# The down projections of two feed-forward blocks and of the last MLP in blocks of 1024 inner by seven half-size products

## The chip, the cores and the metric

The kernel runs on one core of one Trainium2 chip. The metric is the device time of one execution in microseconds (us); the median of three runs is given. A profile of one execution comes with it. The engines are PE (matrix products), DVE (vector), ACT (activation), POOL (GpSimd) and SP, which only issues loads.

## The reference

The reference takes 512 tokens of width 1024 through a state-space mixer, a feed-forward block (FFN), a sparse attention, a second FFN, a hybrid attention, a cross attention and a last MLP. What the change touches is the second matrix product of each of the three feed-forward parts, in float32:

```
gate, up = split(h @ w_gate_up); x = x + (silu(gate) * up) @ w_down     inner width 2816, twice
x = x + relu(h @ w_up)**2 @ w_down_2                                    inner width 4096, once
```

The output width of all three is 1024, so the down weights have 22, 22 and 32 tiles of 128 inner rows.

## The kernel before

**Numbers.** PE takes float32 in a rounded form. Every operand is split in two parts: hi is the value rounded, lo is the rest. `three` (L2180 to L2185) makes one tile of a product by three matmuls: hi by hi, lo of the weights by hi, hi by lo of the activations. All of them run on line L2183.

**Slots.** Weights pass in slots of 128 x 2048 through a pair of buffers: SP loads a slot into `raw` (L456 to L461, two DMAs of 512 KB), ACT rounds it into `w_hi` (L942), POOL subtracts and writes `w_lo` (L682), PE uses it. ACT's rounding of slot g waits for `w_used`, PE's end with slot g - 2; SP's load of slot g waits for the split of slot g - 2. At each of four places where POOL is busy with a norm, DVE splits the slot instead (L1650). Slots are counted in one row through the whole program, 145 of them.

**Up projections.** `t_slot` (L2207) makes 2 output tiles of 128 x 512 (transposed: inner by tokens) with 48 matmuls of 512 columns. In an FFN, one slot gives gate and up of one inner tile: ACT takes silu (L1089), DVE multiplies (L1705), rounds into `hT_hi` (L1707) and subtracts into `hT_lo` (L1709). In the MLP a slot gives two inner tiles: ACT takes relu twice (L1402, L1404), DVE squares 128 x 1024 (L1997), rounds (L1999) and subtracts (L2001). The MLP does 16 inner tiles up, then all 16 down, and this twice (parts); an FFN does 22 up, then 22 down. These loops are hardware loops of two slots (`Fori`).

**Down projections.** `n_slot` (L2187) takes a slot of 3 or 4 inner tiles by 512 output columns; for each of 4 blocks of 128 tokens it makes 3 matmuls per inner tile into one PSUM bank (4 to 7). First all slots of output columns 0 to 511 (a panel), then those of 512 to 1023: 12 slots in an FFN (`FFN_DOWN`), 8 in each part of the MLP. After a panel DVE adds the four banks to the residual `x_res` (L1688).

**The end of an FFN.** The last slot (`n_slot_halves`, L2260) is woven with the next norm. `norm_halves` on DVE (L1645) first splits the next stage's first slot (L1650), then adds token block 0, and so on; ACT squares each block (L986), POOL makes the reciprocal root (L694, L695), DVE and ACT scale the two halves of the block (L1626, L1002), and PE turns it (`half_turn`, L2256) behind blocks 2 and 3 of the last slot. ACT and DVE then copy the turned block into `xT_hi` (L1017) and `xT_lo` (L1641), on which the next stage's first matmuls wait.

**Order.** Each engine works through its own list in order; the order is written out by hand and kept by semaphores.

Of the kernel before, what the change touches and what calls it, by code (L numbers as in the profile page):

```python
# [17 lines left out]
F32R = mybir.dt.float32r  # L18
# [5 lines left out]
P = 128  # L24
# [43 lines left out]
def shape_constants():  # L68
# [61 lines left out]
def program(nc, w, out):  # L130

    with ExitStack() as ctx:
# [44 lines left out]
        sink_e = fixed("sink_e", [P, 8])  # L177
        PS = ctx.enter_context(nc.psum_tensor("PS", [P, 8, 512], F32))
# [2539 lines left out]
```

## Time and profile before

| | |
|---|---|
| median of 3 runs | 1944.69 us (1942.04, 1944.69, 1945.69) |
| the profiled execution: span from the first to the last instruction | 1941.7 us |
| PE busy | 1906.7 us, 98% of the span |
| DVE, ACT, POOL busy | 749.7, 738.5, 811.6 us |
| mean granted TensorE clock | 0.993 |

The profiled execution has no device time of its own on record; its span lies 0.3 us below the fastest and 4.0 us below the slowest of the three runs, and 3.0 us below their median. The profile gives each instruction's start and duration. A matmul's record is longer than its turn: consecutive matmuls overlap, so their pace is read from the distance of their starts, not from the mean duration. Some matmul records can be missing.

### The profile page before, as it was taken

Reading aid. Unit: us, or ns where it says so; the run is one execution under the profiler, and the core shown is the slowest. Engines: PE = TensorE matmul, PEld = TensorE weight load, DVE = VectorE, ACT = ScalarE, POOL = GpSimd, SP = SyncE. Lnnn points to the kernel's source line nnn. Section 1 sums busy time; section 2 is a strip of 40 time slices with the busy share of each in tenths; the row PEclk is TensorE's granted clock in tenths of the full one; section 3 lists DMA queues with packets and bytes.
Section 4 is the critical chain, followed back from the end, with each engine's and each line's share of the span. In section 5 each row is a group of like instructions: output and inputs, shape, how many; then the busy total and the mean of one; then the engine's idle time right before and its main releaser. Section 6 shows DMA issues by size and latency. Waiting matters only on the chain.

```text
span 1941.7 us, 24992 instructions
## 1 busy us (share of the span) xinstructions
PE 1906.7 (98%) x9667; PEld 1541.1 (79%) x9667; DVE 749.7 (39%) x1286; ACT 738.5 (38%) x1141; POOL 811.6 (42%) x411
## 2 busy tenths in 40 slices
PE   7999999999999999999999999999999999999998
PEld 5778888888888878768888888888776778888887
DVE  8973321111003377982211110021636556403721
ACT  6624343222123244683432221243457462212221
POOL 1004344444443458553343434433345444443433
PEclk9999999999999899999999999999999999999999
DMA  6423323332332222103333333335120223323231
GB/s 161 95 51 133 109 77 97 91 103 76 102 103 73 87 65 87 66 2 87 88 86 108 87 95 99 114 86 157 55 66 23 79 64 90 105 88 107 86 108 65
DMA packets 210205, 170.84 MB, mean 88 GB/s; under 512 B 19658, under 2 KB 174746, under 8 KB 210058
## 3 DMA queue, kind: packets, MB, share of 16 engines
q1 hardware_dynamic: 207954, 166.19, 29.2%
q10 hardware_dynamic: 2168, 3.52, 0.5%
q8 instruction: 55, 0.90, 0.2%
q14 instruction: 28, 0.23, 0.0%
HBM read 162.58 MB, written 2.65 MB: 85 GB/s over the span
## 4 chain that ended last, share of the span: by engine, by line
PE 90%; DVE 4%; ACT 4%; issue 1%; DMA 1%; POOL 1%; SPq 0%; POOLq 0%; DVEq 0%; ACTq 0%
PE PS L2183 77%; PE PS L2473 2%; PE PS L2464 2%; PE PS L2483 2%; DMA xp<-in_x 1%; PE PS L2079 1%; PE PS L2100 1%; PE PS L2080 1%; PE PS L2112 1%; DVE taken L1935 1%; PE PS L2426 0%; PE PS L2121 0%; PE PS L2256 0%; ACT probs_t L1232 0%; PE PS L2129 0%
## 5 line engine op out<-in xcount | busy, mean ns | idle before, releaser
L682 POOL TENSOR_TENSOR w_lo<-raw,w_hi 128x2048 fp32r<-128x2048 f32 x141 | 652.0, 4624 | 832.1 <-ACT w_hi L942 830.6
L942 ACT ACTIVATE w_hi<-raw 128x2048 fp32r<-128x2048 f32 x145 | 277.9, 1917 | 630.1 <-PE PS L2183 630.1
L2183 PE MATMUL PS<-xT_hi,w_hi 128*128 128x512 f32 (+1 forms) x1152 | 441.1, 383 | 2.4 <-DVE xT_lo L1641 1.3
L2183 PE MATMUL PS<-xT_lo,w_hi 128*128 128x512 f32 (+1 forms) x1152 | 438.2, 380 | 0.0
L2183 PE MATMUL PS<-xT_hi,w_lo 128*128 128x512 f32 (+1 forms) x1152 | 438.1, 380 | 0.0
L2183 PEld LDWEIGHTS PS<-xT_hi,w_hi 128*128 128x128 f32 x1152 | 216.6, 188 | 49.0 <-issue 7.9
L2183 PEld LDWEIGHTS PS<-xT_lo,w_hi 128*128 128x128 f32 x1152 | 216.6, 188 | 41.5
L2183 PEld LDWEIGHTS PS<-xT_hi,w_lo 128*128 128x128 f32 x1152 | 216.7, 188 | 40.1
L2183 PE MATMUL PS<-w_hi,hT_hi 128*128 128x512 f32 x608 | 236.9, 390 | 0.0
L2183 PE MATMUL PS<-w_hi,hT_lo 128*128 128x512 f32 x608 | 236.6, 389 | 0.0
L2183 PE MATMUL PS<-w_lo,hT_hi 128*128 128x512 f32 x608 | 236.5, 389 | 0.0
L2183 PE MATMUL PS<-w_hi,xT_hi 128*128 128x512 f32 (+2 forms) x592 | 232.0, 392 | 0.9 <-ACT ki_raw L1146 0.7
L2183 PE MATMUL PS<-w_hi,xT_lo 128*128 128x512 f32 (+2 forms) x592 | 228.6, 386 | 0.0
L2183 PE MATMUL PS<-w_lo,xT_hi 128*128 128x512 f32 (+2 forms) x592 | 228.4, 386 | 0.0
L1705 DVE TENSOR_TENSOR gbuf<-gbuf,PS 128x512 f32<-128x512 f32 x44 | 30.3, 689 | 378.8 <-PE PS L2183 378.8
L2183 PEld LDWEIGHTS PS<-w_hi,xT_hi 128*128 128x128 f32 x592 | 114.4, 193 | 29.2 <-issue 8.9
L1688 DVE TENSOR_TENSOR x_res<-x_res,PS 128x512 f32<-128x512 f32 x40 | 27.4, 686 | 279.8 <-PE PS L2183 279.8
L2183 PEld LDWEIGHTS PS<-w_hi,hT_lo 128*128 128x128 f32 x608 | 114.1, 188 | 23.8
L2183 PEld LDWEIGHTS PS<-w_lo,hT_hi 128*128 128x128 f32 x608 | 114.2, 188 | 23.6
L2183 PEld LDWEIGHTS PS<-w_hi,hT_hi 128*128 128x128 f32 x608 | 114.1, 188 | 23.4
L2183 PEld LDWEIGHTS PS<-w_hi,xT_lo 128*128 128x128 f32 x592 | 114.4, 193 | 21.1
L2183 PEld LDWEIGHTS PS<-w_lo,xT_hi 128*128 128x128 f32 x592 | 114.6, 194 | 19.9
(338 smaller groups left out, 2026.2 us busy)
## 6 DMA issues: line engine op xcount, KB each, us to landing
raw<-in_ffn_w_gate_up SPq DMA_DIRECT2D x88, 512.0 KB, 4.6
raw<-in_ffn_w_down SPq DMA_DIRECT2D x40, 512.0 KB, 4.4
raw<-in_w_up SPq DMA_DIRECT2D x32, 512.0 KB, 5.0
raw<-in_w_down SPq DMA_DIRECT2D x32, 512.0 KB, 4.3
raw<-in_dsa_w_in SPq DMA_DIRECT2D x28, 512.0 KB, 4.5
raw<-in_w_in SPq DMA_DIRECT2D x21, 512.0 KB, 4.3
raw<-in_s_w_glu SPq DMA_DIRECT2D x16, 512.0 KB, 4.5
raw<-in_dsa_w_o SPq DMA_DIRECT2D x8, 512.0 KB, 4.6
```

Source lines behind the costliest of these rows:

```text
L682: pool.tensor_tensor(w_lo[:, par, :], raw[:, par, :], f32(w_hi[:, par, :]), ALU.subtract).then_inc(w_split, 1)
L942: act.activation(w_hi[:, par, :], raw[:, par, :], ACT.Copy).then_inc(w_rounded, 1)
L1688: tt(x_res[:, tb, cols], x_res[:, tb, cols], PS[:, 4 + tb, :], ALU.add).then_inc(n_free, 1)
L1705: tt(gbuf[:, pair, 1, :], gbuf[:, pair, 0, :], PS[:, 2 * pair + 1, :], ALU.mult).then_inc(t_free, 1)
L1935: tt(lg[:, :, 0:cols - 1], lg[:, :, 0:cols - 1], rest[:, :, 1:cols], ALU.mult).then_inc(st_prob, 1)
L2079: mm(o, uT[:, GB * b + g, :], tp[:, g, :, :].rearrange("p t h -> p (t h)"), start=True, stop=False)
L2080: ins = mm(o, states[:, g, :], out_a[b % 3][:, g, 1:CH + 1, :].rearrange("p t h -> p (t h)"), start=False, stop=True)
L2100: mm(o, b_n[:, GB * b + g, :], out_a[b % 3][:, g, 0:CH, :].rearrange("p t h -> p (t h)"), start=g % 4 == 0, stop=False)
L2183: ins = mm(o, a if weights_stay else c, c if weights_stay else a, start=first and n == 0, stop=last and n == 2)
L2464: mm(PS[:, dot_bank(u0, t), 0:k.shape[1]], q[half:half + HD], k[half:half + HD], start=True, stop=True).then_inc(col_dot, 1)
L2473: ins = tr(PS[:, 4 + e % 2, P * j:P * j + P], probs[:, e % ring, P * j:P * j + P], ident[:, :])
L2483: ins = mm(PS[HD * i:HD * i + HD, 6 + (p // 4) % 2, at:at + P], units[2 * p + i][3][j], probs_t[:, 2 * (p % 2) + i, P * j:P * j + P], star ...
```

## The change

The inner width is taken in blocks of 8 tiles (1024): two blocks in each FFN (6 tiles are left), three in the MLP (8 tiles are left), seven in all. For a block, tokens (512) are halved, inner (1024) is halved and output columns (1024) are halved. The plain way takes 8 products of 256 tokens x 512 inner x 512 columns; here 7 are taken of sums of the quarters (the scheme of Strassen in the form with 4 sums on each side). A product is 24 matmuls of 128 x 128 by 512 columns (2 token blocks x 4 inner tiles x 3). The tiles that are left over go the old way, in 4 slots per FFN (3 tiles each) and 4 in the MLP (4 tiles each).

- **Where.** A block's 7 products stand between two up slots: the block's last up slot, then one more up slot, then products 0 to 6, then the next up slot. In an FFN a block spans 8 up slots, in the MLP 4. The MLP is no longer in two parts.
- **Loads.** The raw down weights of a block (4 DMAs of 1 MB, `dn_load`) go to a buffer of their own. The first of them waits, from the second block on, until the block before has been split.
- **Weights.** Products 0, 3 and 5 take a raw quarter: ACT rounds it in two halves of 128 x 1024, POOL splits it in two halves. Products 1, 2, 4 and 6 take a sum of quarters: DVE makes the sum (128 x 2048) and splits it, ACT rounds it. The up slot after product 6 is split by DVE (`first_split`), not POOL.
- **Activations.** For each pair of inner tiles DVE makes four sums of 128 x 256 (`pair_sums`), ACT rounds seven pieces of 128 x 256 (`pair_round`: 512, 256 and 1024 wide), DVE subtracts them (`pair_rest`, the same widths).
- **Results.** After each product DVE adds its two banks to `x_res` (`dn_add`, 14 a block). Products 2, 4, 5 and 6 accumulate on a bank that holds an earlier product, so they wait until that one has been added.
- **Loops.** The hardware loops of the three parts are written out. `g_last` has a place of its own; slot numbers shift; `raw` is counted without the products.

The core of the diff (12 columns of indentation are left out):

```diff
-FFN_SLOT = [8, 61]
-FFN_DOWN = [3, 3, 4, 4, 4, 4]
+FFN_RUN, FFN_DN = 8, 2
+FFN_LAST = [3, 3]
+DSA_SLOT = 48
+def up_slot(g0, j, run, dns):
+    return g0 + j + DN * sum(j > run * (c + 1) for c in range(dns))
+def raw_of(g):
+    return g - DN * sum(g > first for first in DN_FIRST)
+DN_PRODUCTS = ("raw", "sum", "sum", "raw", "sum", "raw", "sum")
+DN_QUARTER = {0: (0, 0), 3: (1, 0), 5: (1, 1)}
+DN_SUM = {1: 0, 2: 1, 4: 2, 6: 3}
+DN_ROWS = (0, 3, 4, 1, 5, 6, 2)
+DN_BANK = (4, 6, 4, 0, 4, 6, 4)
+DN_FRESH = (True, True, False, True, False, False, False)
+DN_INTO = ((0, 0), (1, 1), (0, 1), (0, 0), (1, 1), (0, 1), (1, 0))
+DN_BEHIND = (None, None, 0, None, 2, None, 4)
...
-hT_hi = place("hT_hi", "arena", 0, [P, FT, S], F32R)
-hT_lo = place("hT_lo", "arena", FT * S * 4, [P, FT, S], F32R)
-gbuf = place("gbuf", "spare", 0, [P, 2, 2, 512])
+hs_hi = place("hs_hi", "arena", 0, [P, 4, DN, 256], F32R)
+hs_lo = place("hs_lo", "arena", 28 * KB, [P, 4, DN, 256], F32R)
+hT_hi = place("hT_hi", "arena", 16 * KB, [P, 8, S], F32R)
+hT_lo = place("hT_lo", "arena", 32 * KB, [P, 8, S], F32R)
+dn_raw = place("dn_raw", "arena", 56 * KB, [P, 4, 2, 2, 512])
+hid = place("hid", "spare", 0, [P, 2, 512])
+silu = place("silu", "spare", 4 * KB, [P, 2, 512])
+mlp_hid = [hid, silu]
+h_sum = place("h_sum", "spare", 8 * KB, [P, 4, 256])
+sum_b = place("sum_b", "spare", 4 * KB, [P, 4, 512])
...
+def dn_load(cc, src, m):
+    if m == 0 and cc:
+        sp.wait_ge(dn_lo_pool, 6 * cc)
+        sp.wait_ge(dn_sum, 4 * cc)
+    sp.dma_start(dn_raw[:, m, :, :, :].rearrange("p j l n -> p j (l n)"), src).then_inc(dn_ld, 16)
...
+def dn_split(cc, i):
+    g, (j, l) = DN_FIRST[cc] + i, DN_QUARTER[i]
+    for half in range(DN_HALF):
+        ms = slice(2 * half, 2 * half + 2)
+        hi, lo = (t[:, g % 2, 1024 * half:1024 * half + 1024].rearrange("p (m n) -> p m n", n=512) for t in (w_hi, w_lo))
+        pool.wait_ge(dn_hi, 14 * cc + 2 * i + half + 1)
+        pool.tensor_tensor(lo, dn_raw[:, ms, j, l, :], f32(hi), ALU.subtract).then_inc(dn_lo_pool, 1)
...
+def up_splits(g0, run, dns, ups, chunk):
+    for j in range(2, ups):
+        c, at = divmod(j, run)
+        if at == 1 and 1 <= c <= dns:
+            for i in (0, 3, 5):
+                dn_split(chunk + c - 1, i)
+        else:
+            split_run(up_slot(g0, j, run, dns), 1)
...
+def dn_round(cc, i):
+    g = DN_FIRST[cc] + i
+    act.wait_ge(w_used, g - 1)
+    if DN_PRODUCTS[i] == "raw":
+        act.wait_ge(dn_ld, 64 * (cc + 1))
+    else:
+        act.wait_ge(dn_sum, 4 * cc + DN_SUM[i] + 1)
+    for half in range(DN_HALF):
+        ms = slice(2 * half, 2 * half + 2)
+        if DN_PRODUCTS[i] == "raw":
+            src = dn_raw[:, ms, DN_QUARTER[i][0], DN_QUARTER[i][1], :]
+        else:
+            src = (sum_b if DN_SUM[i] % 2 else sum_a)[:, ms, :]
+        act.activation(w_hi[:, g % 2, 1024 * half:1024 * half + 1024].rearrange("p (m n) -> p m n", n=512), src,
+                       ACT.Copy).then_inc(dn_hi, 1)
...
+def pair_round(kk, h):
+    m = kk % 4
+    act.activation(hs_hi[:, m, 0:2, :], h[:, :, 0:256], ACT.Copy)
+    act.activation(hs_hi[:, m, 2, :], h[:, 1, 256:512], ACT.Copy).then_inc(hs_rounded, 1)
+    act.wait_ge(hs_sum, kk + 1)
+    act.activation(hs_hi[:, m, 3:DN, :], h_sum[:, :, :], ACT.Copy).then_inc(hs_rounded, 1)
...
+        next_round(g + 2)
+        if c < FFN_DN and j % 2:
+            act.wait_ge(t_free, t0 + j + 3)
+            pair_round(4 * (c0 + c) + at // 2, hid)
+        if at == 0 and 1 <= c <= FFN_DN:
+            dn_rounds(g0, FFN_RUN, j)
+    g0 += FT + DN * FFN_DN
+    m = len(FFN_LAST)
+    round_run(g0 + 2, m)
     norm_early(1 + 2 * layer, n_free, TB * (FFN_PANEL[layer] + 2))
...
+def pair_sums(kk, h):
+    if kk:
+        dve.wait_ge(hs_rounded, 2 * kk)
+    tt(h_sum[:, 0, :], h[:, 0, 256:512], h[:, 1, 256:512], ALU.add).then_inc(v_step, 1)
+    steps[0] += 1
+    tt(h_sum[:, 2, :], h[:, 0, 0:256], h[:, 0, 256:512], ALU.subtract)
+    dve.wait_ge(v_step, steps[0])
+    link(tt(h_sum[:, 1, :], h_sum[:, 0, :], h[:, 0, 0:256], ALU.subtract))
+    tt(h_sum[:, 3, :], h[:, 1, 0:256], h_sum[:, 1, :], ALU.subtract).then_inc(hs_sum, 1)
+def pair_rest(kk, h):
+    m = kk % 4
+    dve.wait_ge(hs_rounded, 2 * kk + 1)
+    tt(hs_lo[:, m, 0:2, :], h[:, :, 0:256], f32(hs_hi[:, m, 0:2, :]), ALU.subtract)
+    tt(hs_lo[:, m, 2, :], h[:, 1, 256:512], f32(hs_hi[:, m, 2, :]), ALU.subtract)
+    dve.wait_ge(hs_rounded, 2 * kk + 2)
+    dve.wait_ge(hs_sum, kk + 1)
...
+def dn_first_sum(cc):
+        dve.wait_ge(dn_lo_dve, 8 * cc)
...
+def dn_rest(cc, i):
+    g, src = DN_FIRST[cc] + i, sum_b if DN_SUM[i] % 2 else sum_a
+    dve.wait_ge(dn_sum, 4 * cc + DN_SUM[i] + 1)
+    for half in range(DN_HALF):
+        ms = slice(2 * half, 2 * half + 2)
+        hi, lo = (t[:, g % 2, 1024 * half:1024 * half + 1024].rearrange("p (m n) -> p m n", n=512) for t in (w_hi, w_lo))
+        dve.wait_ge(dn_hi, 14 * cc + 2 * i + half + 1)
+        tt(lo, src[:, ms, :], f32(hi), ALU.subtract).then_inc(dn_lo_dve, 1)
...
+def dn_add(cc, i):
+    rows, col = DN_INTO[i]
+    for t in range(2):
+        if t == 0:
+            dve.wait_ge(dn_first, DN * cc + i + 1)
+        else:
+            dve.wait_ge(w_used, DN_FIRST[cc] + i + 1)
+        xs = x_res[:, 2 * rows + t, 512 * col:512 * col + 512]
+        tt(xs, xs, PS[:, DN_BANK[i] + t, :], ALU.add).then_inc(dn_added, 1)
...
+def dn_dve(cc):
+    dve.wait_ge(dn_sum, 4 * cc + 1)
+    dve.wait_ge(hs_done, 4 * cc + 4)
+    tt(sum_b[:, :, :], dn_raw[:, :, 1, 1, :], sum_a[:, :, :], ALU.subtract).then_inc(dn_sum, 1)
+    dn_rest(cc, 1)
+    dn_add(cc, 0)
+    dn_rest(cc, 2)
+    dve.wait_ge(dn_lo_dve, 8 * cc + 2)
+    tt(sum_a[:, :, :], dn_raw[:, :, 1, 1, :], dn_raw[:, :, 0, 1, :], ALU.subtract).then_inc(dn_sum, 1)
+    dn_add(cc, 1)
+    dve.wait_ge(dn_lo_dve, 8 * cc + 4)
+    tt(sum_b[:, :, :], dn_raw[:, :, 1, 0, :], sum_b[:, :, :], ALU.subtract).then_inc(dn_sum, 1)
+    dn_add(cc, 2)
+    dn_rest(cc, 4)
+    dn_add(cc, 3)
+    dn_add(cc, 4)
+    dn_rest(cc, 6)
+    dn_add(cc, 5)
+    first_split(DN_FIRST[cc] + DN)
+    dn_add(cc, 6)
...
-                  norm=6 if part and i else None)
+for j in range(MLP_UP):
+    h = mlp_hid[j % 2]
+    c, at = divmod(j, MLP_RUN)
+    dve.wait_ge(t_free, MLP_TILE + j + 3)
+    tt(h[:, :, :], h[:, :, :], h[:, :, :], ALU.mult).then_inc(hid_made, 1)
+    if at == 0 and 1 <= c <= MLP_DN:
+        dn_dve(MLP_CHUNK + c - 1)
+    dve.wait_ge(hid_made, j + 1)
+    if c < MLP_DN:
+        pair_sums(4 * (MLP_CHUNK + c) + at, h)
+        pair_rest(4 * (MLP_CHUNK + c) + at, h)
+        if at == MLP_RUN - 1:
+            dn_first_sum(MLP_CHUNK + c)
...
+def dn_pe(cc, pair):
+    for i in range(DN):
+        g, c = DN_FIRST[cc] + i, DN_ROWS[i]
+        par = g % 2
+        if i == 0:
+            pe.wait_ge(hs_done, 4 * cc + 4)
+            if cc:
+                pe.wait_ge(dn_added, 14 * cc)
+            pe.wait_ge(n_free, pair[1])
+        if DN_BEHIND[i] is not None:
+            pe.wait_ge(dn_added, 14 * cc + 2 * DN_BEHIND[i] + 2)
+        if i == 3:
+            pe.wait_ge(t_free, pair[0])
+        for half in range(DN_HALF):
+            if DN_PRODUCTS[i] == "raw":
+                pe.wait_ge(dn_lo_pool, 6 * cc + 2 * (0, 3, 5).index(i) + half + 1)
+            else:
+                pe.wait_ge(dn_lo_dve, 8 * cc + 2 * DN_SUM[i] + half + 1)
+            for t in range(2):
+                for m in (2 * half, 2 * half + 1):
+                    cols, rows = slice(512 * m, 512 * m + 512), slice(P * t, P * t + P)
+                    ins = three(PS[:, DN_BANK[i] + t, :], w_hi[:, par, cols], w_lo[:, par, cols],
+                                hs_hi[:, m, c, rows], hs_lo[:, m, c, rows], False,
+                                DN_FRESH[i] and m == 0, DN_FRESH[i] and m == 3, not DN_FRESH[i])
+                if half:
+                    ins.then_inc(w_used if t else dn_first, 1)
...
```

## Rows read from the trace of the kernel before

**Rows 1.** Page, parts 1 and 2: busy time; busy tenths and granted clock in 40 slices

```profile
PE 1906.7 (98%) x9667; PEld 1541.1 (79%) x9667; DVE 749.7 (39%) x1286; ACT 738.5 (38%) x1141; POOL 811.6 (42%) x411
PEclk9999999999999899999999999999999999999999
```

**Rows 2.** Chain of waits in order of time: start, us, what

```profile
251.63 353.38 PE PS L2183 x1590
...
1586.26 348.44 PE PS L2183 x1536
```

**Rows 3.** Groups by form, PE: shapes, count, busy us, mean ns, idle before

```profile
L2183 PE MATMUL PS<-w_hi,hT_hi 128*128 128x512 f32 x608 | 236.9, 390 | 0.0
```

**Rows 4.** Timeline, POOL, the MLP's first slots: start, duration, line, operation

```profile
1599.92 4.69 POOL L682 TENSOR_TENSOR w_lo<-raw,w_hi 128x2048 fp32r<-128x2048 f32 x1 [4.06 <-ACT w_hi L942]
1610.80 4.68 POOL L682 TENSOR_TENSOR w_lo<-raw,w_hi 128x2048 fp32r<-128x2048 f32 x1 [6.19 <-ACT w_hi L942]
```

**Rows 5.** Timeline, DVE, the same stretch

```profile
1598.07 1.22 DVE L1997 TENSOR_TENSOR gbuf<-gbuf 128x1024 f32<-128x1024 f32 x1 [7.35 <-ACT gbuf L1404]
...
1600.27 5.42 DVE L2001 TENSOR_TENSOR hT_lo<-gbuf,hT_hi 128x1024 f32 x1
```

**Rows 6.** Groups by form, DVE: count, busy us, mean ns

```profile
L1709 DVE TENSOR_TENSOR hT_lo<-gbuf,hT_hi 128x512 f32 x44 | 30.5, 693 | 5.4
L1650 DVE TENSOR_TENSOR w_lo<-raw,w_hi 128x2048 fp32r<-128x2048 f32 x4 | 9.2, 2292 | 124.4 <-ACT w_hi L942 124.4
```

**Rows 7.** One line's instructions: duration ns min/median/max (L1676, L942, L682)

```profile
L1676 DVE TENSOR_TENSOR x_res<-x_res,glu_v x16: 424/426/3625, 171.5 to 246.3; 128x256 f32<-128x256 f32 x16
L942 ACT ACTIVATE w_hi<-raw x145: 1894/1916/2003, 148.1 to 1913.0; 128x2048 fp32r<-128x2048 f32 x145
L682 POOL TENSOR_TENSOR w_lo<-raw,w_hi x141: 4517/4623/4940, 150.1 to 1915.0; 128x2048 fp32r<-128x2048 f32 x141
```

**Rows 8.** Timeline, ACT: relu of one tile, turned tiles (six of 128x256)

```profile
1597.44 0.60 ACT L1404 ACTIVATE gbuf<-PS 128x512 f32<-128x512 f32 x1
608.14 2.28 ACT L1017 ACTIVATE xT_hi<-PS,gains 128x256 fp32r<-128x256 f32 x6
```

**Rows 9.** Timeline, PE and DVE, end of a token block in the first FFN

```profile
602.12 0.39 PE L2183 MATMUL PS<-w_hi,hT_hi 128*128 128x512 f32 x1
602.33 0.69 DVE L1688 TENSOR_TENSOR x_res<-x_res,PS 128x512 f32<-128x512 f32 x1 [0.54 <-PE PS L2183]
```

**Rows 10.** Timeline, POOL and DVE, 614 to 620 us

```profile
614.86 4.61 POOL L682 TENSOR_TENSOR w_lo<-raw,w_hi 128x2048 fp32r<-128x2048 f32 x1 [2.64 <-ACT w_hi L942]
616.33 3.23 DVE L1641 SCALAR_TENSOR_TENSOR xT_lo<-PS,gains,xT_hi 128x256 fp32r<-128x256 f32 x8 [3.08 <-ACT xT_hi L1017]
```

**Rows 11.** Timeline, ACT and DVE, the last slot of the first FFN

```profile
596.94 1.92 ACT L942 ACTIVATE w_hi<-raw 128x2048 fp32r<-128x2048 f32 x1 [8.96 <-PE PS L2183]
598.89 2.29 DVE L1650 TENSOR_TENSOR w_lo<-raw,w_hi 128x2048 fp32r<-128x2048 f32 x1 [50.28 <-ACT w_hi L942]
601.10 0.68 DVE L1688 TENSOR_TENSOR x_res<-x_res,PS 128x512 f32<-128x512 f32 x1
603.68 0.71 ACT L1002 ACTIVATE x_n<-x_res,rstd 128x512 f32<-128x512 f32 x1
607.52 0.72 ACT L1002 ACTIVATE x_n<-x_res,rstd 128x512 f32<-128x512 f32 x1 [0.41 <-POOL rstd L695]
```

**Rows 12.** Chain of waits around the same slot's end

```profile
605.01 0.87 PE PS L2256 x8
...
608.32 1.40 PE PS L2183 x6
...
609.98 2.97 PE PS L2183 x12
```

**Rows 13.** DMA issues by line: count, KB each, median us to landing

```profile
raw<-in_w_up SPq DMA_DIRECT2D x32, 512.0 KB, 5.0
w_kv<-in_w_xkv SPq DMA_DIRECT2D x2, 1024.0 KB, 7.6
```

More of the change, by code:

```diff
@@ new lines, in _ @@
+            for j in range(MLP_UP):
+                g = up_slot(MLP_SLOT, j, MLP_RUN, MLP_DN)
+                slot_free(g)
+                load_pair(raw_of(g) % 2, up[:, :, 2 * P * j:2 * P * j + P], up[:, :, 2 * P * j + P:2 * P * j + 2 * P], P)
+                c, m = divmod(j - 1, MLP_RUN)
+                if 0 <= c < MLP_DN:
+                    dn_load(MLP_CHUNK + c, down[:, 8 * c + 2 * m:8 * c + 2 * m + 2, :], m)
+            g = MLP_SLOT + MLP_UP + DN * MLP_DN
+            for i in range(2):
+                k = 8 * MLP_DN
+                for m in MLP_LAST:
+                    slot_free(g)
+                    load_rows(raw_of(g) % 2, down[:, k:k + m, 512 * i:512 * i + 512], 512)
+                    k += m
+                    g += 1
@@ L799, in _ @@
             split_run(XO_SLOT + 2, 1)
[L800 to L805 removed]
+            up_splits(MLP_SLOT, MLP_RUN, MLP_DN, MLP_UP, MLP_CHUNK)
+            split_run(MLP_SLOT + MLP_UP + DN * MLP_DN, 2 * len(MLP_LAST))
             norm_rstd(6)
@@ new lines, in dn_rounds @@
+            def dn_rounds(g0, run, j):
+                c = j // run - 1
+                for i in range(DN):
+                    next_round(dn_slot(g0, c, i, run) + 2)
+            def ffn_act(layer):
+                g0, t0, c0 = FFN_SLOT[layer], FFN_TILE[layer], FFN_CHUNK[layer]
+                for j in range(FT):
+                    n, g = FT * layer + j, up_slot(g0, j, FFN_RUN, FFN_DN)
+                    c, at = divmod(j, FFN_RUN)
+                    act.wait_ge(t_first, t0 + j + 1)
+                    if j >= 2:
+                        act.wait_ge(t_free, t0 + j + 1)
+                    if at == 1 and 1 <= c <= FFN_DN:
+                        act.wait_ge(dn_lo_dve, 8 * (c0 + c))
+                    act.activation(silu[:, j % 2, :], PS[:, 2 * ((t0 + j) % 2), :], ACT.Silu).then_inc(hid_act, 1)
+                    next_round(g + 2)
[4 more added lines that the diff above has]
+                        dn_rounds(g0, FFN_RUN, j)
+                g0 += FT + DN * FFN_DN
+                m = len(FFN_LAST)
+                round_run(g0 + 2, m)
@@ L2365, in ffn_pe @@
             def ffn_pe(layer, n, j0, freed):
-                g0, t0, h0 = FFN_SLOT[layer], FFN_TILE[layer], FFN_HID[layer]
+                g0, t0 = FFN_SLOT[layer], FFN_TILE[layer]
                 t_slot_halves(g0, g0 % 2, t0, n, j0, freed)
-                t_slot(g0 + 1, (g0 + 1) % 2, t0 + 1, 1, xT_hi, xT_lo)
-                with pe.Fori(0, FT // 2 - 1) as i:
-                    for j in range(2):
-                        t_slot(i * 2 + (g0 + j + 2), (g0 + j) % 2, i * 2 + (t0 + j + 2), (t0 + j) % 2, xT_hi, xT_lo)
@@ L2372, in ffn_pe @@
-                g0 += FT
-                m = len(FFN_DOWN)
+                for j in range(1, FT):
+                    c, at = divmod(j, FFN_RUN)
+                    if at == 1 and 1 <= c <= FFN_DN:
+                        dn_pe(FFN_CHUNK[layer] + c - 1, (t0 + j + 2, TB * FFN_PANEL[layer]))
+                    g = up_slot(g0, j, FFN_RUN, FFN_DN)
+                    t_slot(g, g % 2, t0 + j, (t0 + j) % 2, xT_hi, xT_lo)
+                g0 += FT + DN * FFN_DN
+                m = len(FFN_LAST)
```

383 lines of the change are left out of this document (201 added, 182 removed).

## The prediction

> **What bounds the kernel now.** I read the page's busy times first. PE is busy for 98% of the span, DVE and ACT for under 40%, POOL for 42%, and the granted clock stands at the full level but for one slice [rows 1]. So the time is PE's list, and an edit pays by matmuls left out and costs by PE waits brought in. The chain of waits says the same of the stretches that change: the first FFN is one piece of PE work, and so is the whole MLP, 1536 matmuls in 348.44 us, 0.2268 us each [rows 2]. That is the pace; the mean of 390 ns of one record [rows 3] is no turn, since records overlap. As a cross-check, POOL's splits, one a slot, stand 10.88 us apart [rows 4], and 48 matmuls at 0.2268 are 10.89. The written-out code and the two-slot loops both run without gaps there, so writing the loops out is costed at nothing.
>
> **What is removed.** The down products are 608 x 3 = 1824 matmuls [rows 3]. A block takes 7 x 24 = 168 in place of 192. Seven blocks save 168 matmuls, 168 x 0.2268 = **38.1 us**. A product lasts 24 x 0.2268 = 5.44 us, a block's seven 38.1 us. This is all that the change can win; the rest is what comes back.
>
> **Prices.** Of DVE: 128x256 0.42 [rows 7], 128x512 0.69 [rows 6], 128x1024 1.22 [rows 5], 128x2048 2.29 [rows 6], adding a bank 0.69 [rows 9]. Of ACT: 128x256 0.38, 128x512 0.60 [rows 8], 128x2048 1.92 [rows 7], so 128x1024 by the line between the last two 1.04. POOL's 128x2048 split takes 4.62 [rows 7]; a half of 1024 isn't shown: 2.31 if it is all width, 4.62 if none is; it is nearest to the first, and I take 2.4. From a matmul's start to an engine that waits for its end it is about 0.43, which is 0.21 after the next matmul's start [rows 9]; between the other engines I take 0.05.
>
> **The port.** DVE's subtraction of 128x1024 takes 5.42 us in the MLP, while the square of the same size takes 1.22 [rows 5]. It was issued 0.35 us after POOL's split began and ended 1.08 after that split's end [rows 4, 5]. So a DVE instruction with two SBUF inputs stands still while POOL's subtraction runs. One with a PSUM input doesn't: eight of 128x256 ran in 3.23 us inside a POOL split [rows 10]. The change moves DVE work of the first kind beside POOL, so every chain below counts it.
>
> **The layer's end, both FFNs.** The last down slot has 3 inner tiles, before 4. It is 36 matmuls, a token block 9 (2.04 us, before 2.72). But what the turns wait for starts with the slot and has its own length: rounding 1.92, DVE's split 2.29, adding block 0, the square, the root, and block 0 is scaled at 603.68 + 0.71 = 604.39 [rows 11]. Before, PE came for it at 605.01, just later [rows 12]. With the slot's start put at 596.70 (0.24 before the rounding), PE now comes at 596.70 + 27 x 0.2268 = 602.82 and waits until 604.4. Then 6 matmuls (1.4), turn of block 1 at about 606.7 (before 607.26), 3 matmuls. The next stage waits for block 2's scaling (607.52, now about 606.5, since DVE adds block 2 about a microsecond sooner), for ACT's and DVE's copies of the turned halves, and began at 609.98 [rows 11, 12]; it begins about 0.6 sooner, not 2.7. I charge 2.1 us for each FFN, **4.2 us**; bounds 1.6 (the first wait alone) and 2.7 (nothing comes sooner) each.
>
> **Inside a block, MLP.** Time 0 is the end of the block's last up slot; one more up slot follows, so product 0 is due at 10.89. ACT's second relu ends at 0.85, DVE's square at 2.1. ACT has rounded product 0's halves by 2.9, and POOL splits them from 2.1 to 6.9; DVE's four sums wait behind it and end at 8.8. Then the subtractions of 512 and 256 (1.1), ACT's rounding of the sums (1.04, beside them) and the subtraction of 1024 (1.22): 11.1. PE waits **0.3**. DVE next makes the first weight sum (2.29), to 13.4, then slot 4's square, to 14.6, then the second sum, to 16.9, then half of product 1's split, to 18.15. Product 0 ends at 11.2 + 5.44 = 16.6. PE waits **1.6**. After this each sum product's rounding (1.04) and split (2 x 1.22) start when the product two before it ends, with 5.44 us of cover, so they fit, but for one place: POOL's two halves for product 3 and DVE's third sum want the port at the same time, 2.4 + 2.4 + 2.3 in about 6.4 us. One of them is about **0.8** late, product 3's second half or product 4's first. Sum 2.7 a block, **8.1 us** for three.
>
> By the rows alone only DVE waits for POOL: no split of POOL's is above 4.94 [rows 7]. The Trainium skill ("SBUF — State Buffer", Who interferes with whom) says that whichever of the two starts first holds the shared port pair for its whole instruction and the other blocks fully, so POOL would stand behind DVE's sum as well; then it is product 3 that is late, by 0.8, and by the rows alone product 4, by 0.7. The sum is the same within 0.1 a block.
>
> **Inside a block, FFN.** A slot gives one inner tile, so the square is a multiply of 0.69 and the first weight sum is made a slot earlier. The activations are ready at 9.8, before 10.89; product 1's half is ready 0.25 + 0.69 + 0.16 + 2.29 + 1.22 = 4.6 after product 0's start, before 5.44. Only the meeting at product 3 is left, 0.2 to 0.4. **1.6 us** for four blocks.
>
> **What has cover.** ACT rounds 14 halves in a block's 38.1 us, 14.6 us. DVE: 3 x 2.29 + 8 x 1.22 + 14 x 0.69 + 2.29 = 28.6; POOL 6 x 2.4 = 14.4. The slot after product 6 is rounded at product 5's end (1.92), split by DVE (2.29): 4.4 of 5.44. The slot after that has 10.9 us for 1.92 + 4.6. If a product were a microsecond shorter, these would be late next. On SP's queue the block's first load waits for POOL's last half of the block before, and the next up slot's load stands behind it: issued about 10 us before its rounding, with 1 MB landing in 5.0 to 7.6 us [rows 13] twice in a row, 10 to 15; up to 3 late at ACT, and POOL's split still ends within the 10.9 us of the slot before. PE's added waits (16 and more a block) cost nothing when met: down slots in the MLP have four waits more than up slots and run in the one gapless piece [rows 2].
>
> **Sum.** -38.1 + 4.2 + 8.1 + 1.6 = **-24.2 us**. The profiled span becomes 1941.7 - 24.2 = 1917.5; it lies 3.0 below the median of the runs, so the median becomes 1944.69 - 24.2 = **1920.5**.
>
> **Rivals.**
> - *The waits are covered.* If POOL and DVE interleave better than I drew it (sums slip between POOL's halves), only the layers' ends come back: -33.9, 1910.8. For it: DVE, ACT and POOL are idle most of the time [rows 1]. Against: the port row. Chance 0.12, for 1906 to 1914.
> - *Each hand-over is dearer.* A POOL half of 2.9 and 0.15 between engines: in the same drawing the MLP blocks wait 5.3 us each and the FFN's 1.2, together 21; 33.9 - 21 = 13 is left, 1932. For it: margins of 1 us or less at products 0, 1, 3 and at the slot behind. Against: the rows agree to 0.1 us from slot to slot [rows 4]. Chance 0.18, for 1926 to 1941.
> - *DVE becomes the bound (slower).* Place: DVE's list in the blocks. If POOL stops all of it, the adds too, a block needs 28.6 + 14.4 = 43.0 us of both, 4.9 over PE's 38.1; DVE also stands before four roundings (4.2) and starts late (1.9): 11 a block, 77 in all, against 33.9: +43, 1988. It decides from 33.9 / 7 = 4.8 us a block. Against: the PSUM-fed instructions that ran beside a split [rows 10]. Chance 0.07.
> - *Nothing is left over*, by waits of just that size: 0.02. That the products aren't fewer is excluded by the loops of the diff.
>
> **Numbers.** My forecast, 1914 to 1926, has 0.61. A measurement of this kernel tells about 0.2% (4 us) from no change. Faster 0.91, within 0.2% 0.02, slower 0.07. The range takes in the covered case from 1909 and the dearer one up to 1936.
>
> **What would show it.** Down matmuls: 1656, of them 1176 in products, at a pace of 0.227. PE idle, or late starts, before products 0 and 1 in the MLP, put down to DVE, 0.3 and 1.6; in the FFNs almost none. DVE sums of 128x256 with a maximum above 2 us. The turn of token block 0 at the FFN's end starting late, the next stage 0.6 us sooner after the last slot's start. It would be wrong if the products ran at another pace or clock, or if blocks wait over 4 us.

## The result and the profile after

| | before | changed |
|---|---|---|
| median of 4 runs each | 1944.28 us | 1913.74 us |
| all runs | 1944.69, 1945.69, 1942.04, 1943.86 | 1912.14, 1912.0, 1915.52, 1915.33 |
| span of the profiled execution | 1941.7 us | 1910.3 us |
| PE, DVE, ACT, POOL busy | 1906.7, 749.7, 738.5, 811.6 us | 1869.4, 1071.4, 808.4, 771.0 us |

The changed kernel takes 0.9844 of the time before (95% interval 0.983 to 0.9858), 30.5 us less by the medians. The profiled executions differ by 31.4 us, and the account below is of these.

The page of the changed kernel, busy times and granted clock, answering to [rows 1]:

```profile
PE 1869.4 (98%) x9499; PEld 1507.3 (79%) x9499; DVE 1071.4 (56%) x1575; ACT 808.4 (42%) x1275; POOL 771.0 (40%) x418
PEclk9999999999999899999999999999999999999999
```

PE is still the bound and its share has not moved. DVE is busy for 322 us more. Its record counts the time it stands still at the port, so this is more than its work.

The chain of waits of the changed kernel, its pieces in order of time (start, length, what), answering to [rows 2]. The first two lines are the FFNs, the rest is the MLP, of whose four pieces the third is left out:

```profile
252.12 337.50 PE PS L2410 x1518
918.56 337.45 PE PS L2410 x1518
1567.73 43.83 PE PS L2410 x192
1628.40 65.80 PE PS L2410 x288
...
1793.66 109.30 PE PS L2410 x480
```

The FFN pieces are still whole. An FFN piece now ends at the start of the last slot. From there on the chain runs through ACT and DVE. So the piece has 72 matmuls fewer: 48 that the two blocks save, and 24 because it leaves out all 36 of the last slot, where before it left out 12. By the pace that is 353.38 - 72 x 0.2268 = 337.05 us, and 0.4 more was measured. The MLP runs from 1567.73 to 1793.66 + 109.30 = 1902.96, so 335.2 us, cut three times, once in each block. Its ideal is 348.44 - 72 x 0.2268 = 332.1, so 3.1 us came back.

Set side by side by the starts of stages in the two chains, the 31.4 us are:

| stretch | before | changed | difference |
|---|---|---|---|
| up to the first FFN's long piece | 251.63 | 252.12 | +0.5 |
| first FFN, up to the next stage's first matmul | 358.35 | 349.70 | -8.65 |
| sparse attention | 318.41 | 316.74 | -1.7 |
| second FFN, likewise | 358.39 | 349.71 | -8.7 |
| up to the MLP | 299.48 | 299.46 | 0.0 |
| MLP | 348.44 | 335.23 | -13.2 |
| rest | 7.0 | 7.3 | +0.3 |

An FFN saves 48 matmuls, 10.9 us, and keeps 8.7. The MLP saves 72, 16.3 us, and keeps 13.2. The 1.7 us of the sparse attention did not need the products; "All else" below says where they come from.

**The products.** The page's groups of the changed kernel (line, engine, operation, count | busy, mean ns | idle before, and what ended it):

```profile
L2410 PE MATMUL PS<-w_hi,hs_hi 128*128 128x512 f32 x392 | 153.6, 392 | 1.6 <-DVE w_lo L1866 1.6
...
L754 POOL TENSOR_TENSOR w_lo<-dn_raw,w_hi 128x1024 fp32r<-128x1024 f32 x42 | 116.7, 2800 | 182.3 <-ACT w_hi L1169 182.3
```

With the groups of `w_lo` by `hs_hi` and `w_hi` by `hs_lo`, 392 each too, the products are 3 x 392 = 1176 matmuls. POOL's half takes 2800 ns in the mean; one alone takes 2392, as its line's minimum shows:

```profile
L754 POOL TENSOR_TENSOR w_lo<-dn_raw,w_hi x42: 2392/2449/4482, 337.4 to 1814.0; 128x1024 fp32r<-128x1024 f32 x42
```

**Where PE waits for the blocks.** Waits of PE and of its weight loads in the changed kernel (us in total, times, longest):

```profile
PE PS L2483 <- ACT x_n L1075: 3.1, 2, 1.5
PE PS L2410 <- DVE w_lo L1866: 1.6, 3, 0.5
PEld PS L2410 <- DVE w_lo L1866: 2.9, 3, 1.0
PEld PS L2410 <- POOL w_lo L754: 2.3, 7, 0.3
```

There are three kinds. The turn of block 0 is late at the end of each FFN. In each of the three MLP blocks, product 1 waits for DVE's subtraction. In all seven blocks, a weight load waits up to 0.3 us for POOL, before product 3's second half. No line names product 0.

**Inside an MLP block.** The chain of waits of the changed kernel in the first block, from DVE's first sum of activations to product 1:

```profile
1613.48 2.52 DVE h_sum L1833
1615.99 2.53 DVE h_sum L1835
1618.52 0.35 DVE h_sum L1837
...
1621.59 1.54 DVE sum_a L1856
...
1625.09 2.04 issue
1627.13 1.23 DVE w_lo L1866
1628.40 1.65 PE PS L2410 x6
```

POOL's timeline of the same stretch (start, busy, what, idle before):

```profile
1613.21 5.03 POOL L754 TENSOR_TENSOR w_lo<-dn_raw,w_hi 128x1024 fp32r<-128x1024 f32 x2 [5.39 <-ACT w_hi L1169]
```

POOL runs its two halves from 1613.21 to 1618.24. Two of DVE's four sums of 128x256, 0.42 us alone, take 2.5 each there: each stands behind one half. The other two take 0.4. The prediction had all four behind both halves. The 2.04 us of "issue" are no wait: DVE makes the second weight sum (2.28) there. Product 0 was over at 1627.71, and product 1 began at 1628.40.

**At the FFN's end.** The chain of waits of the changed kernel, from the rounding of the next stage's first slot to its first matmul, answering to [rows 11, 12]:

```profile
589.70 1.93 ACT w_hi L1015
591.64 2.29 DVE w_lo L1778
...
594.57 0.73 ACT sq_junk L1059 x2
595.46 0.28 POOL rstd L761
...
596.38 0.73 ACT x_n L1075
597.25 1.06 PE PS L2483 x8
...
601.82 3.00 PE PS L2410 x12
```

With the slot's start at 589.46 (0.24 before the rounding, as in the prediction), block 0's turn starts 7.8 us into the slot and the next stage 12.36 into it, where it was 609.98 - 596.70 = 13.28. It gains 0.9 of 2.72. The second FFN does the same.

### The profile page after: what moved, and what is told of

Read it like the earlier page. It is cut to its first block, busy times and chain, and to the rows that moved or that the text cites. A ratio compares the mean times of both kernels' runs of the same rounds, so it can differ in the third digit from the quotient of the medians.

```text
span 1910.3 us, 23860 instructions
## 1 busy us (share of the span) xinstructions
PE 1869.4 (98%) x9499; PEld 1507.3 (79%) x9499; DVE 1071.4 (56%) x1575; ACT 808.4 (42%) x1275; POOL 771.0 (40%) x418
## 4 chain that ended last, share of the span: by engine, by line
PE 86%; DVE 6%; ACT 4%; issue 2%; DMA 1%; POOL 1%; SPq 0%; POOLq 0%; DVEq 0%; ACTq 0%
PE PS L2410 74%; PE PS L2731 2%; PE PS L2722 2%; PE PS L2741 2%; DMA xp<-in_x 1%; PE PS L2339 1%; PE PS L2306 1%; PE PS L2327 1%; PE PS L2307 1%; DVE taken L2157 1%; PE PS L2684 0%; PE PS L2348 0%; PE PS L2483 0%; ACT probs_t L1352 0%; PE PS L2356 0%
## 5 line engine op out<-in xcount | busy, mean ns | idle before, releaser
L745 POOL TENSOR_TENSOR w_lo<-raw,w_hi 128x2048 fp32r<-128x2048 f32 x106 | 493.0, 4651 | 668.8 <-ACT w_hi L1015 667.4
L1015 ACT ACTIVATE w_hi<-raw 128x2048 fp32r<-128x2048 f32 x117 | 224.2, 1917 | 400.5 <-PE PS L2410 400.5
L1920 DVE TENSOR_TENSOR hid<-silu,PS 128x512 f32<-128x512 f32 x44 | 30.3, 688 | 286.5 <-PE PS L2410 286.5
L754 POOL TENSOR_TENSOR w_lo<-dn_raw,w_hi 128x1024 fp32r<-128x1024 f32 x42 | 116.7, 2800 | 182.3 <-ACT w_hi L1169 182.3
L2410 PE MATMUL PS<-w_hi,hs_hi 128*128 128x512 f32 x392 | 153.6, 392 | 1.6 <-DVE w_lo L1866 1.6
L2410 PE MATMUL PS<-w_lo,hs_hi 128*128 128x512 f32 x392 | 152.6, 389 | 0.0
L2410 PE MATMUL PS<-w_hi,hs_lo 128*128 128x512 f32 x392 | 152.6, 389 | 0.0
L856 POOL TENSOR_TENSOR inv_sum<-row_sum,minus_one 128x1 f32<-128x1 f32 x128 | 73.0, 580 | 63.5 <-ACT probs L1341 53.8
L2410 PEld LDWEIGHTS PS<-w_hi,hs_hi 128*128 128x128 f32 x392 | 73.6, 188 | 20.1 <-DVE w_lo L1866 2.9
L1877 DVE TENSOR_TENSOR x_res<-x_res,PS 128x512 f32<-128x512 f32 x98 | 65.2, 683 | 42.9 <-PE PS L2410 42.9
```

The costliest lines, as they stand in the source:

```text
L745: pool.tensor_tensor(w_lo[:, g % 2, :], raw[:, r % 2, :], f32(w_hi[:, g % 2, :]), ALU.subtract).then_inc(w_split, 1)
L754: pool.tensor_tensor(lo, dn_raw[:, ms, j, l, :], f32(hi), ALU.subtract).then_inc(dn_lo_pool, 1)
L856: pool.tensor_tensor(inv_sum[:, c], row_sum[:, c], minus_one[:, 0:1], ALU.pow).then_inc(col_inv, 1)
L1015: act.activation(w_hi[:, g % 2, :], raw[:, r % 2, :], ACT.Copy).then_inc(w_rounded, 1)
L1877: tt(xs, xs, PS[:, DN_BANK[i] + t, :], ALU.add).then_inc(dn_added, 1)
L1920: tt(hid[:, j % 2, :], silu[:, j % 2, :], PS[:, 2 * pair + 1, :], ALU.mult).then_inc(t_free, 1)
```

## The experiments

Ten runs were made, in three groups, each beside runs of the kernel before on its chip (medians 1943.54 of 7, 1944.22 of 8, 1944.09 of 9). Unless said otherwise an edit is to the changed kernel. Ratios are to the kernel before.

| run | median us | ratio (95%) |
|---|---|---|
| e5_raw_on_dve | 1910.2 | 0.9826 (0.981 to 0.9843) |
| e2_sum_early | 1912.33 | 0.9838 (0.9821 to 0.9854) |
| e4_third_sum_late | 1910.81, one run | |
| e6_two_mlp_blocks | 1916.88 | 0.9859 (0.9842 to 0.9875) |
| e3_add_first | 1913.3 | 0.9843 (0.9826 to 0.9859) |
| e8_scale_first | 1912.09 | 0.9839 (0.9823 to 0.9854) |
| e9_dve_and_scale | 1908.38 | 0.9814 (0.98 to 0.9827) |
| e9b, the same kernel again | 1907.92 | 0.9813 (0.98 to 0.9827) |
| e10_split_in_halves | 1908.66 | 0.981 (0.9797 to 0.9824) |
| e1_unrolled (of the kernel before) | 1942.02, one run | |

Most medians lie within 3 us of their neighbours, so the verdicts rest on the pieces of the chain. Where nothing was edited these agree from run to run to a few hundredths, but for one piece in the sparse attention, whose clock differs (see "All else"). Through it the spans and medians differ by a further 1.5 to 3.1 us, so they are not to be read to the microsecond.

**e5_raw_on_dve: is it the port?** The raw quarters are split by DVE, and POOL does nothing in a block:

```diff
-                        for i in (0, 3, 5):
-                            dn_split(chunk + c - 1, i)
+                        pass
...
                 dn_add(cc, 1)
+                dn_split(cc, 3)
...
                 dn_add(cc, 3)
+                dn_split(cc, 5)
...
+                    if at == MLP_RUN - 1:
+                        dn_split(MLP_CHUNK + c, 0)
                     pair_sums(4 * (MLP_CHUNK + c) + at, h)
```

> The changed kernel, but the raw quarters of products 0, 3 and 5 are split on DVE (6 x 1.22 us a block more there), not on POOL, which has nothing to do in a block. Theory A (DVE is late at product 1 because it stands still behind POOL's two halves of product 0, 4.8 us, at the port): the four sums of the last pair run in 0.42 us each in the FFNs and the MLP but for up slots' splits, product 0's split takes 2.4 in place of 4.8, product 1 starts in turn in the MLP; DVE's list in a block is 28.6 + 7.3 = 35.9 of 38.1 us and still fits: the whole 1 to 3 us faster than the changed kernel. Theory B (DVE's list is the bound in a block, the port is nothing): each block is 1 us or more longer, 7 us or more slower in all.

The chain of waits of this kernel:

```profile
252.63 337.07 PE PS L2415 x1518
...
1568.89 332.53 PE PS L2415 x1464
```

The MLP is one piece of 332.53, against the ideal of 332.1 and 335.2 in the changed kernel. The FFN pieces stand at the ideal, 337.07. 3.5 of the 3.9 us that the blocks gave back are gone, though DVE has 6 more subtractions of 1.2 us in each block. The edit also changes how long a raw half takes, 1.22 us on DVE for 2.39 on POOL. But product 1, which was late by most of the MLP's 3.1 us, uses nothing that POOL makes: POOL can have delayed it only by holding up DVE, as the two sums of 2.5 us show. So it was the meeting of the two engines that cost, and not the work on DVE's list.

**e2_sum_early: is it the place of the first weight sum?** In the MLP it is made a slot earlier:

```diff
-                    if at == MLP_RUN - 1:
+                    if at == MLP_RUN - 2:
                         dn_first_sum(MLP_CHUNK + c)
```

> The changed kernel, but in the MLP the first weight sum of a block is made one up slot earlier (behind the block's third up slot, as the FFNs have it). Theory A (PE's lost time in an MLP block is the wait before product 1, and that comes from DVE's list, in which the weight sum of 2.29 us stands ahead of the square and the second sum): product 1 starts in turn, 5.44 us after product 0, and the MLP, from its first matmul's start to its last one's end, goes from 335.2 to about 332.7 us (3 blocks x 0.84). Theory B (the 1.04 us a block is PE's own price of the waits and bank changes in the products, spread over them): the MLP stays at 335.2. Theory C (the sum only moves the conflict with POOL's split to the slot before, and the activations come later): product 0 is late instead, 335 or more.

The chain of waits of this kernel, before product 0 of the first block:

```profile
1611.00 1.42 DVE sum_a L1856
1613.20 1.23 DVE silu L2215
...
1621.42 1.24 DVE hs_lo L1848
1622.70 9.36 PE PS L2410 x40
```

The MLP took 334.0 us, 1.2 less than before the edit. Product 1 comes in its turn, as the theory has it, but the sum's 2.29 us now stand ahead of the square, and product 0 is late instead. So the wait before product 1 does come from DVE's list, as expected; but a slot earlier the sum is in the way as well, and 1.2 of the expected 2.5 us came.

**e4_third_sum_late: is it DVE's third sum that makes product 3 late?** It is moved past product 4's split, away from POOL's halves for product 3:

```diff
-                dve.wait_ge(dn_lo_dve, 8 * cc + 4)
-                tt(sum_b[:, :, :], dn_raw[:, :, 1, 0, :], sum_b[:, :, :], ALU.subtract).then_inc(dn_sum, 1)
                 dn_add(cc, 2)
                 dn_rest(cc, 4)
+                dve.wait_ge(dn_lo_dve, 8 * cc + 4)
+                tt(sum_b[:, :, :], dn_raw[:, :, 1, 0, :], sum_b[:, :, :], ALU.subtract).then_inc(dn_sum, 1)
```

> The changed kernel, but DVE makes the last weight sum of a block (for product 6) behind product 4's split, not before product 2's result is added. Theory A (POOL's second half for product 3 is late because it stands behind this sum at the port, 4.5 us instead of 2.4; this is the 0.2 us a block that the FFNs lose): no POOL half above 3.6 us, the FFNs go from 337.45 to 337.1 us from the first full-width stretch's start to the last slot's, the MLP from 335.2 to 334.7. Theory B (0.2 a block is the price of starting products at all): both stay.

POOL's splits of this kernel (ns, minimum/median/maximum):

```profile
L754 POOL TENSOR_TENSOR w_lo<-dn_raw,w_hi x42: 2394/2412/2604, 337.5 to 1812.6; 128x1024 fp32r<-128x1024 f32 x42
```

The maximum falls from 4482 to 2604 ns. Both FFN pieces became 337.07, so their 0.4 each is gone, and the MLP took 1792.45 + 109.15 - 1566.99 = 334.6, 0.6 less for three blocks. So the late half of product 3 was POOL standing behind DVE's sum, and it cost 0.2 a block.

**e6_two_mlp_blocks: what is a block worth?** The MLP has two blocks, and 16 of its inner tiles go the old way:

```diff
-MLP_RUN, MLP_DN, MLP_UP = 4, 3, 16
-MLP_LAST = [4, 4]
+MLP_RUN, MLP_DN, MLP_UP = 4, 2, 16
+MLP_LAST = [4, 4, 4, 4]
...
```

> The changed kernel, but the MLP takes two blocks of 1024 inner by seven products and 16 inner tiles the old way (three and 8 before): one block fewer. Theory A (a block is worth 24 matmuls x 0.2268 = 5.44 us less 1.04 of waits): the MLP goes from 335.2 to 339.6 us. Theory B (what is lost is not lost in the blocks but once, where the MLP's pattern changes): 340.6 us.

The MLP in the chain of waits of this kernel, its first and last piece:

```profile
1568.57 43.80 PE PS L2414 x192
...
1711.85 196.37 PE PS L2414 x864
```

It took 1711.85 + 196.37 - 1568.57 = 339.65, 4.4 more than with three blocks. A block wins 5.44 by its 24 matmuls and gives back 1.0 in the MLP. That is the first theory's 339.6 and not the second's 340.6: the loss stands in the blocks. The medians differ by 3.1.

**e3_add_first: is DVE's split ahead of the first add what delays the turn?** At the FFNs' ends block 0 is added before the split:

```diff
+                if n in (1, 3):
+                    add(0)
                 first_split(FIRST_SLOTS[n])
-                add(0)
+                if n not in (1, 3):
+                    add(0)
```

> The changed kernel, but at the end of both FFNs DVE adds token block 0 before it splits the next stage's first slot, not after. Theory A (the last slot of 36 matmuls no longer covers the chain rounding, split, add, square, root, scaling): the first turn comes in its place, 6.1 us after the slot's start instead of 7.8, and the next stage starts 10.9 us after the slot's start instead of 12.4, about 1.4 us sooner in each FFN, 2.8 in all. Theory B (the chain of blocks 1 and 2 is as long, so the first turn's wait only moves to the second): less than 0.5 us in each.

ACT's timeline of this kernel:

```profile
592.54 0.63 ACT L1059 ACTIVATE sq_junk<-x_res 128x512 f32<-128x512 f32 x1 [0.79 <-DVE x_res L1823]
...
595.34 0.63 ACT L1059 ACTIVATE sq_junk<-x_res 128x512 f32<-128x512 f32 x1 [2.08 <-DVE x_res L1823]
...
595.97 0.71 ACT L1075 ACTIVATE x_n<-x_res,rstd 128x512 f32<-128x512 f32 x1
```

Block 0 is squared 2 us sooner, but the turn only 0.6: it starts 7.2 us into the slot and the next stage 11.79, before 12.36. ACT's list has block 1's square ahead of block 0's scaling, and that square now waits for DVE's second add, which waits behind the split. The wait moved from one engine's order to another's. The gain of 0.6 is near the under 0.5 of the second theory, but its reason, the length of block 1's and block 2's chains, was not the one.

**e8_scale_first: e3, and ACT scales block 0 before it squares block 1.**

```diff
                     square_row(n, tb, sem_x, value)
-                    if tb:
+                    if n in (1, 3) and tb == 0:
+                        right_row(n, 0)
+                    if tb == 2 or tb == 1 and n not in (1, 3):
                         right_row(n, tb - 1)
```

> As the run with block 0 added first, and in both FFNs' ends ACT scales token block 0 before it squares block 1. Theory A (in that run the first turn still waited because ACT's list has the square of block 1 ahead of block 0's scaling, and that square waits for DVE's split): the first turn starts in its place, 6.1 us after the last slot's start (7.2 in that run, 7.8 in the changed kernel), and the next stage 11.0 us after it instead of 12.4: about 1.3 us sooner in each FFN, 2.7 in all. Theory B (block 2's chain sets the next stage's start whatever comes before): 11.8, as in that run.

POOL's timeline of this kernel:

```profile
592.93 1.41 POOL L761 TENSOR_SCALAR rstd<-ssq,rstd 128x1 f32<-128x1 f32 x1 [4.87 <-ACT sq_junk L1059]
...
596.43 0.27 POOL L761 TENSOR_SCALAR rstd<-ssq,rstd 128x1 f32<-128x1 f32 x1 [1.47 <-ACT sq_junk L1059]
```

The next stage begins 11.66 us into the slot (589.09 to 600.75), not 11.0. POOL's step on 128x1 takes 1.41 us where the next takes 0.27. It ended at 594.34, and DVE's split (591.92, 2.29 long) at 594.21. So even a step of one element per partition seems to stand behind a DVE subtraction; e10 tries it.

**e10_split_in_halves: is that so?** In e9 (e5 and e8 together) DVE's split at the FFNs' ends is cut in two halves, with block 1's add between them:

```diff
-                first_split(FIRST_SLOTS[n])
+                    half_split(FIRST_SLOTS[n], 0)
...
                 add(1)
+                    half_split(FIRST_SLOTS[n], 1)
```

> The fastest kernel so far (raw quarters split on DVE; at the FFNs' ends block 0 added before DVE's split and scaled before block 1 is squared), and in the same two places DVE's split of the next slot made in two halves of 1.22 us, one before and one after block 1 is added. Theory A (POOL's small step for block 0's root, 0.28 us, took 1.42 there because it stood behind DVE's split of 2.29 at the port): the step takes under 0.5, the first turn starts 6.1 us after the last slot's start instead of 6.8, the next stage 11.0 to 11.2 instead of 11.7: 0.5 us sooner in each FFN, 1 us in all. Theory B (the step was long for its own sake): nothing changes.

The same step in POOL's timeline of this kernel:

```profile
592.34 0.34 POOL L752 TENSOR_SCALAR rstd<-ssq,rstd 128x1 f32<-128x1 f32 x1 [4.87 <-ACT sq_junk L1049]
```

It takes 0.34 and ends at 592.68, again 0.13 behind the DVE subtraction beside it (591.33, 1.22 long). So the step was long because of DVE, and not of itself. The next stage begins 588.51 to 599.82 = 11.31 into the slot, against 11.64 in e9b; 11.0 to 11.2 was expected. The turn now waits for DVE's own scaling, which stands behind the second half of the split. The 0.7 us that the two FFNs gain are not seen in the medians: in the profiles the sparse attention of e10 took 1.5 us more than that of e9b, by its clock.

**e9_dve_and_scale: do the two gains add?** It is e5 and e8 together:

> Raw quarters split on DVE as in the run before, together with the new order at the ends of the FFNs (DVE adds token block 0 before it splits the next slot; ACT scales block 0 before it squares block 1). If the two causes (POOL's hold on the port in the blocks, ACT's and DVE's order at the layer's end) are separate, their gains add: 3.5 us from the first and 2.7 from the second, about 6 us below the changed kernel, 1907.5. If they are not, under 4.

> The fastest kernel so far once more, beside the one with the split in halves: within 1 us of its first median, 1908.4.

It took 1908.38 and, again on another chip, 1907.92, each some 36 us below the kernel before and 5.4 and 5.8 below the changed one. Its MLP took 332.56 in both profiles. By the pieces the gains add: the MLP and the two FFNs are 4.9 us shorter than in the changed kernel, where e5 alone gave 3.5 and e8 alone 1.5 (and not the 2.7 that was expected of it). This is the best version that was run, with e10 as its equal within the measurement.

**e1_unrolled: does writing the loops out cost or bring anything?** The hardware loops of the kernel before are written out, nothing else:

```diff
-with ... .Fori(0, ...) as i:
+for i in range(...):
```

> The kernel before with all its hardware loops written out, nothing else. Theory A (writing out costs and gains nothing on PE's path, as costed): MLP 348.4 us, FFN stretches 353.4, the time within 3 us of the kernel before; the table loads of ACT in the FFN loops (1.28 us each) disappear, but they stood in idle time. Theory B (the written-out code brings waits for instructions, or frees some): more than 1 us in one of these stretches.

The chain of waits of this kernel:

```profile
251.92 353.38 PE PS L2183 x1590
...
1584.77 348.42 PE PS L2183 x1536
```

The pieces are those of [rows 2] to 0.02 us, so writing the loops out was rightly costed at nothing. The kernel's one run lies 2.2 us below the median before; its sparse attention is 1.8 us shorter, by its clock.

## Why the prediction was right

The forecast was 1920.5, and 1913.74 was measured. The sign held, and so did the main term, the matmuls left out, and the kind of each wait; the gain came out 6.8 us larger than forecast. The time lies within the whole range of 1909 to 1936, but 0.3 us below the 1914 to 1926 that had a chance of 0.61: it fell into the interval of a rival that had 0.12. By the same account as the prediction's sum, in the profiled executions:

| term | predicted | measured |
|---|---|---|
| 168 matmuls at 0.2268 | -38.1 | -38.1 (1176 in products; in e5 the FFN pieces are at the ideal, the MLP 0.4 above) |
| the layers' ends | +4.2 | +3.6 |
| MLP blocks | +8.1 | +3.1 |
| FFN blocks | +1.6 | +0.8 |
| all else | 0 | -0.9 |
| sum (terms rounded) | -24.2 | -31.4 |

- **The bound and the gain** were right: the pace, the count, no cost of the loops.
- **The MLP blocks** are the term that was mis-sized. The step that failed is "DVE's four sums wait behind it and end at 8.8". Two of them slip between POOL's halves, the sums end at 8.1, and the activations are ready 10.3 us after the last up slot, not 11.1. So product 0's wait of 0.3 is gone, and product 1's is 0.7 and not 1.6. Some 0.3 of the gain before product 1 is the step from one DVE instruction to the next: each starts about 0.08 before the recorded end of the one before, and the prediction's sums of durations counted these overlaps. The mechanism behind "the waits are covered" (sums slip between the halves) was thus half true, and the time, 1913.74, lies at the edge of that rival's 1906 to 1914. The prediction wrote this as all or nothing; what came was in between.
- **The FFN blocks** cost 0.8 and not 1.6. Only product 3 was late there, as predicted; the sum took the top of its own 0.2 to 0.4 a block, and 0.2 was measured.
- **Product 3 or 4.** The rows alone had only DVE wait. The trace shows the two engines taking turns, POOL's first half, DVE's third sum, POOL's second half, and it is product 3 that is late. POOL's and DVE's timelines of the changed kernel:

```profile
1635.32 6.84 POOL L754 TENSOR_TENSOR w_lo<-dn_raw,w_hi 128x1024 fp32r<-128x1024 f32 x2 [17.07 <-ACT w_hi L1169]
1636.27 3.61 DVE L1891 TENSOR_TENSOR sum_b<-dn_raw,sum_b 128x2048 f32<-128x2048 f32 x1
```

  The sum, 2.29 alone, waits for the first half, and the second half, 2.39 alone and 4.48 here, for the sum. So the rule of the Trainium skill ("SBUF — State Buffer", Who interferes with whom), that whoever starts first holds the port pair and the other blocks fully, agrees with this trace, and e4 with its 2604 ns for 4482 bears it out. The size was 0.2 and not 0.8, of which 0.07 is lateness and the rest the slower start below. The three instructions took 6.84 us in the 6.8 up to the half's turn (1635.32 to 1642.14), where the prediction drew 7.1 in 6.4.
- **The layers' ends** were right in kind: PE waits for block 0's scaling, 1.5 us each. The next stage came 0.9 sooner and not 0.6.
- **The rivals.** "Each hand-over is dearer" fell: a POOL half alone is 2.39, not 2.9, and the hand-overs of the MLP block's chain took 0.02 to 0.04. "DVE becomes the bound" fell by e5: with all of POOL's part on it DVE still keeps up with PE. "Nothing is left over" fell by the 30.5 us.

**All else.** The sparse attention ran 1.7 us shorter, with no edit in it, less 0.5 and 0.3 at the start and the end. Its first long piece, 174 matmuls, carries 1.3 of that. The chain of waits of the kernel before:

```profile
616.07 34.23 PE PS L2183 x174
```

of the changed one:

```profile
607.94 32.92 PE PS L2410 x174
```

and the window from 606 to 700 us (length, busy us of PE, PEld, DVE, ACT and POOL, granted clock, DMA) of the kernel before, then of the changed one:

```profile
606.00:700.00 94.00, 93.09 (x443) 73.02 (x442) 43.59 (x81) 35.71 (x64) 40.62 (x20) 0.91 0.21 67
```

```profile
606.00:700.00 94.00, 93.35 (x453) 73.56 (x452) 48.04 (x92) 33.90 (x56) 44.65 (x18) 0.93 0.22 72
```

The windows' clocks are means, and the piece has a different place in each. In windows of 4 us the granted clock is at 1.00 or at 0.50, the lower of its two levels (1.2 for 2.4 GHz), but for the windows in which it changes. Added up, it stands at the lower level for 17.0 us in the kernel before (from about 638 to 655) and for 13.6 in the changed one (631 to 645). It falls in both while PE works on 96 narrow matmuls of 72 columns, which began at 633.7 and 625.6. PE has no wait but one of 0.65 us there, so 3.4 us less at half the clock are worth 1.7 us: all of the difference in the sparse attention.

The twelve profiles have one of three lengths:

| at the lower level | sparse attention | kernels |
|---|---|---|
| 13.6 to 13.7 us | 316.6 to 316.7 us | changed, e1, e2, e4, e8 |
| 17.0 to 17.1 us | 318.2 to 318.4 us | before, e3, e5, e6, e9, e9b |
| 20.5 us | 319.8 us | e10 |

That e1, the kernel before with its loops written out, has the shortest shows that the products are not needed for it. So as far as these runs show, these 1.7 us of the profiled difference are not the change's doing, and a larger miss by them is chance. One kernel may have several: the four runs of the changed kernel lie at 1912.0 and 1912.1 with a mean granted clock of 0.994, and at 1915.3 and 1915.5 with 0.992, and only the first of them was traced. What picks the length was not tried and stays open.

**By the profiles** the miss is 7.2 us: 5.0 in the MLP blocks, 1.4 in the other two terms, 0.9 in all else (rounded). By the medians it is 6.8.

## What to carry to other kernels

Price a meeting of two engines at a shared port by its order, instruction by instruction: an instruction that stands between two of the other engine's pays for one of them, not for the sum. Where moving work to a second engine makes it meet the first at the port, try leaving it on the first: here DVE with all the blocks' splits was faster than DVE and POOL together, 1910.2 us for 1913.74. When a wait is taken away, look at the next entry of each engine's list (ACT's square, POOL's step of 128x1) before counting the gain.

## What the runs showed of the hardware

- A POOL step on 128x1 took 0.27 us alone and 1.41 beside a DVE subtraction with two SBUF inputs (e8), 0.34 when that subtraction was half as long (e10). In both it ended 0.13 us behind the subtraction's end.
- A POOL subtraction of 128x1024 took 2.39 us alone and 4.48 behind DVE's sum of 128x2048; a DVE sum of 128x256 took 0.42 us alone and 2.5 behind such a POOL half.
- PE's granted clock fell to 1.2 GHz for 13.6, 17.0 or 20.5 us in a stage that no edit touched, and the stage took 316.7, 318.3 or 319.8 us.

PE starts slowly after a wait. PE's timeline of the changed kernel at product 1:

```profile
1628.40 0.50 PE L2410 MATMUL PS<-w_hi,hs_hi 128*128 128x512 f32 x1 [0.53 <-DVE w_lo L1866]
1628.74 0.40 PE L2410 MATMUL PS<-w_lo,hs_hi 128*128 128x512 f32 x1
1628.98 0.39 PE L2410 MATMUL PS<-w_hi,hs_lo 128*128 128x512 f32 x1
```

The starts stand 0.34 and 0.24 apart, and only then at the pace of 0.227, so this wait of 0.69 us cost about 0.12 us more than its length. The second half of product 3 came 0.07 us late (at 1642.21) and its first starts stand 0.34 and 0.23 apart, so a wait ten times shorter cost as much. It is most of what product 3 lost.

The kernel before loads ACT's table on its silu line 22 times, 28.2 us in all on ACT; with the loops written out (e1) it does so twice, and the FFN and MLP pieces of the chain changed by no more than 0.02 us. So these loads had cover.
